# A hybrid decoder trunk: the attention layer in sixteen units of a quarter of the tokens and one head, and weights and rows loaded ahead of the stage borders

## Chip, cores and metric

One core of a Trainium2 chip runs the whole program as one launch. The metric is the device time of one execution in microseconds (us). All work is float32. Matrix products are made of three passes over operands that were split into a high and a low part (fp32r): high x high, high x low, low x high.

## What is computed

```python
def reference(x, ...):                      # x: 1 x 2048 x 1024
    x = x + gla_mixer(x, ...)               # layer 0
    x = x + hier_moe(x, ...)
    x = x + rglru_mixer(x, ...)             # layer 1
    x = x + hier_moe(x, ...)
    return rmsnorm(x, final_norm)

def gla_mixer(x, ...):                      # 4 heads, keys 128, values 256, chunks of 64 tokens
    q, k, v, g, lr = split(rmsnorm(x) @ w_in)
    log_a = log_sigmoid(lr @ w_alpha + b_alpha) / 16
    cum = cumsum(log_a within a chunk)
    q_in, k_in = q * exp(cum - mid), k * exp(mid - cum)
    o = causal(q_in @ k_in.T) @ v + (q * exp(cum)) @ state
    state = exp(last) * state + (k * exp(last - cum)).T @ v
    return (rmsnorm(o per head) * silu(g)) @ w_out

def hier_moe(x, ...):                       # 4 groups of 8 experts, hidden 256
    h = rmsnorm(x)
    group = argmax(h @ w_group); top 2 of its 8 experts by h @ w_expert
    return weighted sum of (silu(h @ w_gate) * (h @ w_up)) @ w_down over the two
```

`rglru_mixer` is a convolution over four tokens, two gates of 256 x 256 blocks, a linear recurrence over the tokens and two projections.

## The kernel before, in words

Seven stages run one after the other: `gla`, `project_and_route` (layer 0), `experts`, `lru`, `project_and_route` (layer 1), `experts`, `finish`. Each stage has its own memory, its own semaphores and a barrier at its end, and nothing of a stage is loaded before the stage begins. Every stage is written as one program for each engine (SyncE issues loads and stores, ScalarE, VectorE, TensorE, GpSimd the gathers), and each of them works strictly in the order of its lines; they meet through semaphores. SyncE first primes most semaphores (`m.prime`), so that loops may wait for an index below zero.

**gla** (line 264) works on two halves of 1024 tokens. At the start of a half all eight tiles of 128 tokens are loaded, normalised (`Norm`, squares and root on ScalarE, L259 the product on VectorE), transposed on TensorE (L685) and split into `hT_hi` and `hT_lo`; then come two low-rank projections `lr` (L693, 24 products each). Behind that is a loop over four heads. A head has two groups of 512 tokens:

- TensorE projects Q, K (24 products of 512 columns each, L710) and the decay logits (L714) for both groups. ScalarE copies Q and K out of PSUM and makes the softplus in four steps (L466 to L473); VectorE sums up (`sum_up`, L585 to L592); ScalarE makes five exponentials (L481 to L485); VectorE multiplies them with Q and K (`decay`, L596 to L612).
- Per tile TensorE makes values and gates together (24 products, L118 to L120 of `matmul3`), the scores (L747 to L751), and for the tile before the outputs and the update of the state (L725 to L728). ScalarE copies the values (L502) and squares the outputs (`square_o`, L417); VectorE takes the scores (L619 to L624), the outputs and the state (L629, L631).
- After four tiles the outputs are gated: silu (L517) and a root on ScalarE, the product on VectorE (L640); TensorE transposes them (L672, eight products), in the second tile of the next group, or at once for the second group of a head; ScalarE takes them (`take_oT`, L425), SyncE stores them.

The raw weights of a head lie in one buffer, `w_raw`: first Q and K (2048 columns a partition), split in ScalarE's L411 and VectorE's L544, then values and gates (4096 columns). Each head's weights are thus loaded and split twice, once in each half.

**project_and_route** projects with `w_out` (L118, weights split in four parts, L963), adds the residual, normalises, computes router logits and, on VectorE in small steps each of which waits for the one before, chooses experts and places each token in a list (`choose` 15 steps, `place_tokens` 14 steps, L1001 to L1034). **experts** loads the weights of 32 experts through two buffers, splits them (L1343, L1384) and runs over blocks of gathered rows. **lru** adds the two expert rows to x (L1747) and works in sixteen steps. **finish** adds the expert rows of the second MoE and normalises (L1967, L248), four tiles to an iteration of a loop.

Of the kernel before, what the change touches and what calls it, by code (L numbers as in the profile page):

```python
# [30 lines left out]
P = 128  # L31
BANK = 512
START = 4
DMA = 16
# [133 lines left out]

def stand(eng):


    eng.nop(nofuse=True)
# [91 lines left out]
def gla(nc, k, x_dram, norm_w, w_in, w_alpha, b_alpha, head_norm, oT_dram):  # L264
# [3 lines left out]

    with ExitStack() as ctx:
        m = Memory(nc, ctx, "gla")
        hT_hi = m.sb("hT_hi", [P, KD, TH], F32R)
        hT_lo = m.sb("hT_lo", [P, KD, TH], F32R)  # L280
        work = m.sb("work", [P, 4, D])
        q_k = m.sb("q_k", [P, 2 * GROUP])
        q_sb, k_sb = q_k[:, 0:GROUP], q_k[:, GROUP:]
        norm = Norm(m, k, work[:, 0:2], work[:, 2:4], q_k[:, 0:D])

        vg = work[:, 0:2].rearrange("p a (b c) -> p (a b) c", c=2 * DV)
        o_raw = work[:, 2].rearrange("p (a c) -> p a c", c=DV)
        gated = work[:, 3].rearrange("p (a c) -> p a c", c=DV)


# [10 lines left out]
        wal_in, wal = m.sb("w_alpha_in", [RANK, DK]), m.sb("w_alpha", [RANK, DK])  # L301
        bal_in, bal = m.sb("b_alpha_in", [P, 1]), m.sb("b_alpha", [P, 1])
        hn = m.sb("head_norm", [P, DV // P])
        lrT = m.sb("lrT", [RANK, TH])

        q_in, k_in, q_x, k_x, q_dec, k_dec = (m.sb(s, [P, NG, GROUP]) for s in (
            "q_in", "k_in", "q_x", "k_x", "q_dec", "k_dec"))
        tile_decay = m.sb("tile_decay", [P, NG, GT])
# [10 lines left out]
        oss = m.sb("oss", [P, GT])  # L319
        ostd = m.sb("ostd", [P, GT])  # L320
        orstd = m.sb("orstd", [P, GT])
# [6 lines left out]
        hT_ps_done, hT_hi_done, hT_lo_done = m.sem("hT_ps_done"), m.sem("hT_hi_done"), m.sem("hT_lo_done")  # L328
        small_in = m.plain("small_in")
        wlr_done, zeroed = m.plain("wlr_done"), m.plain("zeroed")  # L330
        wqk_in, wvg_in = m.plain("wqk_in"), m.plain("wvg_in")
        wqk_hi_done, wqk_lo_done = m.sem("wqk_hi_done"), m.sem("wqk_lo_done")
        wvg_hi_done, wvg_lo_done = m.sem("wvg_hi_done"), m.sem("wvg_lo_done")
        lr_ps_done, lrT_done = m.sem("lr_ps_done"), m.sem("lrT_done")
        qkz_ps_done = m.sem("qkz_ps_done")
        soft_steps = m.sem("soft_steps")
        cum_done, exps_done, group_done = m.sem("cum_done"), m.sem("exps_done"), m.sem("group_done")
        vg_ps_done, vg_done = m.sem("vg_ps_done"), m.sem("vg_done")
        sc_ps_done, sc_done = m.sem("sc_ps_done"), m.sem("sc_done")
        ou_ps_done = m.sem("ou_ps_done")  # L340
        o_raw_done, state_done = m.sem("o_raw_done"), m.sem("state_done")
        oss_done, ostd_done = m.sem("oss_done"), m.sem("ostd_done")
        og_done, oT_ps_done, oT_done = m.sem("og_done"), m.sem("oT_ps_done"), m.sem("oT_done")
        oT_stored = m.store("oT_stored")
# [6 lines left out]

        @block.sync
        def _(sp):
            m.prime(sp)

            def load_qk(h):
                sp.dma_start(wqk_raw[:, :, 0:DK], w_rows[:, :, bass.ds(h * DK, DK)]).then_inc(wqk_in, DMA)
                sp.dma_start(wqk_raw[:, :, DK:], w_rows[:, :, bass.ds(h * DK + KC, DK)]).then_inc(wqk_in, DMA)
                sp.dma_start(wal_in[:], w_alpha[:, bass.ds(h * DK, DK)]).then_inc(wqk_in, DMA)
                with nc.allow_non_contiguous_dma(reason="128 biases"):  # L360
                    sp.dma_start(bal_in[:], b_alpha.rearrange("(c o) -> c o", o=1)[bass.ds(h * DK, DK), :])\
                        .then_inc(wqk_in, DMA)

            def load_vg(h):
                sp.dma_start(wvg_raw[:, :, 0:DV], w_rows[:, :, bass.ds(h * DV + VC, DV)]).then_inc(wvg_in, DMA)
                sp.dma_start(wvg_raw[:, :, DV:], w_rows[:, :, bass.ds(h * DV + GC, DV)]).then_inc(wvg_in, DMA)

            for i in range(2):
                sp.dma_start(norm.x[:, i], x_dram[i * P:(i + 1) * P, :]).then_inc(x_in[i], DMA)
            sp.dma_start(norm.norm_w[:], norm_w.partition_broadcast(P)).then_inc(norm.norm_w_in, DMA)  # L370
            sp.dma_start(wlr_raw[:], w_rows[:, :, LC:LC + RANK]).then_inc(small_in, DMA)
            with nc.allow_non_contiguous_dma(reason="256 gains"):
                sp.dma_start(hn[:], head_norm.rearrange("(h p) -> p h", p=P)).then_inc(small_in, DMA)
            load_qk(0)
            sp.wait_ge(wqk_lo_done, nth(0))
            load_vg(0)
            with sp.Fori(0, HALVES) as half:
                for i in range(2, HT):
                    sp.wait_ge(norm.h_done, nth(half * HT + (i - 2)))
                    sp.dma_start(norm.x[:, i % 2], x_dram[bass.ds(half * TH + i * P, P), :])\  # L380
                        .then_inc(x_in[i % 2], DMA)
                with sp.Fori(0, HEADS) as h:
                    n = half * HEADS + h


                    sp.wait_ge(wvg_lo_done, nth(n))
                    load_qk((h + 1) % HEADS)
                    sp.wait_ge(wqk_lo_done, nth(n + 1))
                    load_vg((h + 1) % HEADS)
                    for g in range(NG):  # L390
                        sp.wait_ge(oT_done, nth(n * NG + g))
                        for e in range(DV // P):
                            sp.dma_start(oT_dram[bass.ds(h * DV + e * P, P),
                                                 bass.ds(half * TH + g * GROUP, GROUP)],
                                         oT[:, e]).then_inc(oT_stored, DMA)


                for i in range(2):
                    sp.dma_start(norm.x[:, i], x_dram[bass.ds(((half + 1) % HALVES) * TH + i * P, P), :])\
                        .then_inc(x_in[i], DMA)  # L400
            sp.wait_ge(oT_stored, nth_store(HALVES * HEADS * NG * (DV // P) - 1))
            sp.wait_ge(wqk_in, nth_dma(4 * HALVES * HEADS + 3))
            sp.wait_ge(wvg_in, nth_dma(2 * HALVES * HEADS + 1))
            for i in range(2):
                sp.wait_ge(x_in[i], nth_dma(HALVES * HT // 2))

        @block.scalar
        def _(act):
            def split_qk(n):
                act.wait_ge(wqk_in, nth_dma(4 * n + 3))  # L410
                nc.scalar.activation(wqk_hi[:], wqk_raw, ACT.Copy).then_inc(wqk_hi_done, 1)  # L411

            def square_o(i, t):

                act.wait_ge(oss_done, nth(t - 1))
                act.wait_ge(o_raw_done, nth(t))
                nc.scalar.activation(o_square[:], o_raw[:, i], ACT.Square,  # L417
                                     accum_out=oss[:, i:i + 1]).then_inc(oss_done, 1)
# [1605 lines left out]
```

## Time and profile before

| | us |
|---|---|
| median of three runs | 3212.1 (3206.96 to 3215.69) |
| the profiled execution | 3209.87 |
| its span | 3208.1 |
| gla ends | 868.6 |
| project_and_route (layer 0) ends | 1156 |
| experts (layer 0) ends | 1714 |
| lru ends | 2279 |
| project_and_route (layer 1) ends | 2557 |
| experts (layer 1) ends | 3096 |
| TensorE busy | 2677.0 (83%) |
| VectorE busy | 1824.7 (57%) |
| ScalarE busy | 1626.1 (51%) |
| GpSimd busy | 588.3 (18%) |
| DMA, busiest of 40 slices | 342 GB/s |

The ends are those of the last instruction of a stage; in gla the first transposes on TensorE start at 24.6. The mean granted clock of TensorE over the span is 0.925 of its full 2.4 GHz. PE is TensorE's matrix product, DVE is VectorE, ACT is ScalarE. A busy share is a mean over stages with different limits, so the table only says where to look.

### The profile page before, as it was taken

Reading aid. Unit: us, or ns where it says so; the run is one execution under the profiler, and the core shown is the slowest. Engines: PE = TensorE matmul, PEld = TensorE weight load, DVE = VectorE, ACT = ScalarE, POOL = GpSimd, SP = SyncE. Lnnn points to the kernel's source line nnn. Section 1 sums busy time; section 2 is a strip of 40 time slices with the busy share of each in tenths; the row PEclk is TensorE's granted clock in tenths of the full one; section 3 lists DMA queues with packets and bytes.
Section 4 is the critical chain, followed back from the end, with each engine's and each line's share of the span. In section 5 each row is a group of like instructions: output and inputs, shape, how many; then the busy total and the mean of one; then the engine's idle time right before and its main releaser. Section 6 shows DMA issues by size and latency. Waiting matters only on the chain. (4 is left out here: it accounts for less than half of the span.)

```text
span 3208.1 us, 43209 instructions
## 1 busy us (share of the span) xinstructions
PE 2677.0 (83%) x12246; PEld 2126.9 (66%) x12246; DVE 1824.7 (57%) x3426; ACT 1626.1 (51%) x2253; POOL 588.3 (18%) x795
## 2 busy tenths in 40 slices
PE   4999969999789949999993999999599588999940
PEld 3777756777678837777772777777488466777730
DVE  3444443434356656657653688886466667656645
ACT  3445444444334436556653666666344266555533
POOL 0000000000001134545450000000011144545420
PEclk9999979999989979999996999999799789999975
DMA  3111121111154359888876445422444299977857
GB/s 102 44 46 52 35 83 39 32 47 52 59 199 144 124 197 325 282 281 293 299 245 223 163 167 172 167 99 86 159 138 144 86 342 342 314 253 262 288 224 274
DMA packets 358416, 552.11 MB, mean 172 GB/s; under 512 B 32128, under 2 KB 273936, under 8 KB 354192
## 3 DMA queue, kind: packets, MB, share of 16 engines
q1 hardware_dynamic: 323296, 436.20, 41.1%
q0 software_dynamic: 32688, 105.99, 8.8%
q10 hardware_dynamic: 2304, 8.39, 0.6%
q8 instruction: 58, 0.95, 0.1%
q14 instruction: 70, 0.57, 0.0%
HBM read 428.29 MB, written 122.22 MB: 172 GB/s over the span
## 5 line engine op out<-in xcount | busy, mean ns | idle before, releaser
L1384 DVE TENSOR_TENSOR experts_gu_lo<-experts_gu_raw,experts_gu_hi 128x1024 fp32r<-128x1024 f32 x256 | 296.5, 1220 | 83.8 <-ACT experts_gu_hi L1343 82.1
L118 PE MATMUL experts_ps<-experts_gu_hi,experts_hT_hi 128*128 128x512 f32 x760 | 318.3, 419 | 0.5 <-DVE experts_hT_lo L1395 0.5
L1266 POOL DMA_INDIRECT experts_rows<-h_rows,experts_source_now x194 | 261.9, 1350 | 273.8 <-PE experts_ps L1436 136.7
L119 PE MATMUL experts_ps<-experts_gu_lo,experts_hT_hi 128*128 128x512 f32 x760 | 301.7, 397 | 0.0
L120 PE MATMUL experts_ps<-experts_gu_hi,experts_hT_lo 128*128 128x512 f32 x760 | 299.9, 395 | 0.0
L1343 ACT ACTIVATE experts_gu_hi<-experts_gu_raw 128x1024 fp32r<-128x1024 f32 x256 | 249.9, 1055 | 74.2 <-DMA experts_gu_raw<-in_moe_w_up 74.2
L892 POOL MEMSET route_empty<- 128x512 int32 x2 | 1.1, 549 | 1445.0 <-POOLq L160 1445.0
L118 PE MATMUL route_ps<-route_w_hi,route_src_hi 128*128 128x512 f32 x512 | 213.1, 416 | 60.6 <-DVE route_w_lo L963 60.6
L1395 DVE TENSOR_TENSOR experts_hT_lo<-experts_ps,experts_hT_hi 128x512 fp32r<-128x512 f32 x194 | 132.9, 686 | 225.1 <-ACT experts_hT_hi L1322 223.8
L118 PE MATMUL gla_ps<-gla_wvg_hi,gla_hT_hi 128*128 128x512 f32 x512 | 212.1, 414 | 0.0
L1335 ACT ACTIVATE experts_y<-experts_ps,experts_by_block 128x1024 f32<-128x1024 f32 x99 | 110.6, 1117 | 199.0 <-DMA y_rows<-experts_y,experts_target_now 198.8
L119 PE MATMUL route_ps<-route_w_lo,route_src_hi 128*128 128x512 f32 x512 | 207.7, 406 | 0.0
L120 PE MATMUL route_ps<-route_w_hi,route_src_lo 128*128 128x512 f32 x512 | 207.2, 405 | 0.0
L118 PE MATMUL experts_ps<-experts_wd_hi,experts_aT_hi 128*128 (+1 forms) x396 | 174.3, 440 | 34.2 <-DVE experts_aT_lo L1400 28.7
L120 PE MATMUL gla_ps<-gla_wvg_hi,gla_hT_lo 128*128 128x512 f32 x512 | 202.6, 396 | 0.0
L119 PE MATMUL gla_ps<-gla_wvg_lo,gla_hT_hi 128*128 128x512 f32 x512 | 201.6, 394 | 0.0
L1436 PE MATMUL experts_ps<-ident,experts_rows 128*128 128x128 f32 x776 | 122.5, 282 | 93.3 <-DMA experts_rows<-h_rows,experts_source_now 92.5
L1436 PEld LDWEIGHTS experts_ps<-ident,experts_rows 128*128 128x128 f32 x776 | 93.3, 143 | 137.1 <-issue 113.1
L120 PEld LDWEIGHTS experts_ps<-experts_gu_hi,experts_hT_lo 128*128 128x128 f32 x760 | 143.2, 188 | 35.2
L119 PE MATMUL experts_ps<-experts_wd_lo,experts_aT_hi 128*128 (+1 forms) x396 | 163.6, 413 | 0.0
L120 PE MATMUL experts_ps<-experts_wd_hi,experts_aT_lo 128*128 (+1 forms) x396 | 163.4, 413 | 0.0
L118 PEld LDWEIGHTS experts_ps<-experts_gu_hi,experts_hT_hi 128*128 128x128 f32 x760 | 144.1, 190 | 27.4 <-DVE experts_hT_lo L1395 0.7
(300 smaller groups left out, 6528.1 us busy)
## 6 DMA issues: line engine op xcount, KB each, us to landing
experts_gu_raw<-in_moe_w_gate SPq DMA_DIRECT2D x64, 1024.0 KB
experts_gu_raw<-in_moe_w_up SPq DMA_DIRECT2D x64, 1024.0 KB
experts_wd_raw<-in_moe_w_down SPq DMA_DIRECT2D x64, 1024.0 KB, 5.7
gla_w_raw<-in_gla_w_in SPq DMA_DIRECT2D x18, 1024.0 KB, 6.6
route_src<-oT_rows SPq DMA_DIRECT2D x32, 512.0 KB, 4.3
x_rows<-route_x_new SPq DMA_DIRECT2D x32, 512.0 KB, 2.9
h_rows<-route_h SPq DMA_DIRECT2D x64, 256.0 KB, 2.3
lru_y_ab<-y_rows SPq DMA_DIRECT2D x16, 1024.0 KB, 7.6
```

The source lines that it names most:

```text
L118: nc.tensor.matmul(out, w_hi, x_hi, start=first, stop=False)
L119: nc.tensor.matmul(out, w_hi, x_lo, start=False, stop=False)
L120: return nc.tensor.matmul(out, w_lo, x_hi, start=False, stop=last)
L892: pool.memset(empty[:, :, 1], 0)
L1266: pool.indirect_dma_start(rows[:, b], None, h_halves[b], bass.IndirectOffsetOnAxis(source_now[b][:].bitcast(U32), 0))\
L1335: nc.scalar.activation(y[:].rearrange("p (b c) -> p b c", b=2), ps[:, Y:Y + 2], ACT.Copy, scale=by_block[:, bass.ds(i + (LAG - 2), 1), 1]. ...
L1343: nc.scalar.activation(gu_hi[:, slot(e), of_part(c)], gu_raw[:, slot(e), of_part(c)], ACT.Copy)\
L1384: nc.vector.tensor_tensor(gu_lo[:, slot(e), of_part(c)], gu_raw[:, slot(e), of_part(c)], gu_hi[:, slot(e), of_part(c)].bitcast(F32), ALU.s ...
L1395: nc.vector.tensor_tensor(hT_lo[:, of_half(b)], ps[:, HT_ + b].rearrange("p (a c) -> p a c", c=P), hT_hi[:, of_half(b)].bitcast(F32), ALU. ...
L1436: last = nc.tensor.transpose(ps[:, HT_ + b, c * P:(c + 1) * P], rows[:, b, c * P:(c + 1) * P], k.ident[:])
```

## The change

`gla` is written anew and unrolled. It goes over sixteen units; unit u is quarter u // 4 of the tokens (512 of them, four tiles) and head u % 4.

- Only the first four tiles are normalised and transposed in front. The others follow one in each unit: in unit u, tile u + 4 is normalised at the end of the unit before, transposed after the first tile's scores, and split. `hT` has two buffers of a quarter each. The low-rank product of the next quarter stands in a quarter's last unit.
- Q and K of the next unit are projected at the end of a unit, its decay logits in the unit's second tile, its softplus and `sum_up` after the third tile. VectorE reads Q and K straight from PSUM. Output transposes stand in the second tile of the next unit; the silu covers all four tiles.
- Weights are loaded and split in every unit, so sixteen times each instead of eight. Values and gates are split in four parts of 1024 columns.
- gla's semaphores aren't primed.

TensorE's new order:

```python
for u in range(UNITS):                                   # 16
    ahead = u + GT
    for i in range(GT):                                  # 4 tiles
        t = GT * u + i
        values(t)
        if i == 1 and ahead < NT and u % HEADS == HEADS - 1:
            after(pe, hT_lo_done, ahead)
            low_rank(u // HEADS + 1)
        scores(t)
        if i:
            outputs(t - 1)
        if i == 0 and ahead < NT:
            transpose(ahead, Q)
        if i == 1:
            if ahead < NT:
                after(pe, hT_lo_done, ahead)
            if u:
                transpose_outputs(u - 1)
            if u + 1 < UNITS:
                decay_logits(u + 1)
    if u + 1 < UNITS:
        after(pe, oT_done, u - 1)
        project(u + 1, Q, 0, q_ps_done)
    outputs(t)
    if u + 1 < UNITS:
        project(u + 1, K, DK, k_ps_done)
```

VectorE's (ScalarE's mirrors it, with `square_o(t - 1)` ahead of `split_qk(u + 1)`, which stands ahead of `take_oT(u - 1)`; `soften(u + 1)` ahead of `mean_square` and `root_mean` of the next tile; then `gate(u)`, `decays(u + 1)`, `split_vg(u + 1)`, `square_o` and `root_o`):

```python
for u in range(UNITS):
    ahead = u + GT
    split_vg(u)
    if u:
        take_outputs(GT * u - 1)
    decay(u)
    if u:
        gate_outputs(u - 1)
    for i in range(GT):
        t = GT * u + i
        take_scores(t)
        if i:
            take_outputs(t - 1)
        if i == 0 and ahead < NT:
            take_hT(ahead, Q)
        if i == 1 and u + 1 < UNITS:
            split_qk(u + 1)
        if i == 2 and u + 1 < UNITS:
            sum_up(u + 1)
    if ahead + 1 < NT:
        normalise(ahead + 1)
```

TensorE, second tile of a group, before (group 1 of a head; `gla_work` holds values and gated outputs):

```order
L747 MATMUL gla_ps<-gla_q_in,gla_k_in 128x128 [waits gla_sc_done]
L749 MATMUL gla_ps<-gla_q_x,gla_k_x 128x64
L751 MATMUL gla_ps<-ident,gla_k_dec 128x128
L725 MATMUL gla_ps<-gla_work,gla_sT 128x256 [waits gla_o_raw_done,gla_state_done,gla_vg_done,gla_sc_done]
L726 MATMUL gla_ps<-gla_state,gla_q_dec 128x256
L728 MATMUL gla_ps<-gla_work,gla_kd 128x256
L757 ISA
L672 MATMUL gla_ps<-ident,gla_work 128x128 [waits gla_og_done]
L672 MATMUL gla_ps<-ident,gla_work 128x128 x7
L118 MATMUL gla_ps<-gla_wvg_hi,gla_hT_hi 128x512 [waits gla_vg_done]
```

and after, second tile of a unit:

```order
L756 MATMUL gla_ps<-gla_q_in,gla_k_in 128x128 [waits gla_sc_done,gla_group_done]
L757 MATMUL gla_ps<-gla_q_x,gla_k_x 128x64
L758 MATMUL gla_ps<-ident,gla_k_dec 128x128
L767 MATMUL gla_ps<-gla_vg,gla_sT 128x256 [waits gla_o_raw_done,gla_state_done,gla_vg_done,gla_sc_done]
L768 MATMUL gla_ps<-gla_state,gla_q_dec 128x256
L770 MATMUL gla_ps<-gla_vg,gla_kd 128x256
L776 MATMUL gla_ps<-ident,gla_gated 128x128 [waits gla_og_done,gla_hT_lo_done]
L776 MATMUL gla_ps<-ident,gla_gated 128x128 x7
L732 MATMUL gla_ps<-gla_lrT,gla_w_alpha 128x512 [waits gla_wqk_lo_done,gla_soft_steps,gla_lrT_done]
L118 MATMUL gla_ps<-gla_wvg_hi,gla_hT_hi 128x512 [waits gla_vg_done]
```

The decay logits (L732) moved in between the output transposes and the next tile's values, with a wait for the low part of the next unit's Q and K weights.

VectorE, from a unit's third tile to the next unit's decays, after:

```order
L614 SCALAR_TENSOR_TENSOR gla_cum<-keep,gla_z 128x512 [waits gla_exps_done,gla_vector_order]
L618 TENSOR_TENSOR gla_soft<-gla_cum 128x512 [waits gla_vector_order]
L619 TENSOR_TENSOR gla_to_end<-gla_cum 128x512
L651 COPY gla_kd<-gla_ps 128x128 [waits gla_sc_ps_done,gla_ou_ps_done]
L654 COPY_PREDICATED gla_sT<-causal,gla_ps 64x64 x2
L655 COPY gla_sT<-gla_ps 64x64
L660 COPY gla_o_raw<-gla_ps 128x256 [waits gla_ou_ps_done]
L662 SCALAR_TENSOR_TENSOR gla_state<-gla_state,gla_tile_decay,gla_ps 128x256 [waits gla_ou_ps_done]
L577 RECIPROCAL gla_rstd<-gla_std 128x1 [waits gla_std_done]
L579 SCALAR_TENSOR_TENSOR gla_h<-gla_x,gla_rstd,gla_gain 128x1024 [waits gla_hT_ps_done,gla_vector_order]
L599 TENSOR_TENSOR gla_wvg_lo<-gla_w_raw,gla_wvg_hi 128x1024 [waits gla_wvg_hi_done] x4
L660 COPY gla_o_raw<-gla_ps 128x256 [waits gla_ou_ps_done]
```

The sums of the next unit stand ahead of the fourth tile's scores, and the four parts of the value weights ahead of the last tile's outputs; before, sums, decays and the split stood at the head of a head, in front of its first scores.

At the stage borders:

- An arena (`Carry`, allocated once) holds in turn gla's first `hT` buffer, the raw `w_out` of a route stage, the raw gate and up weights of the experts, and lru's first `hT` buffer. With it, loads move ahead: `w_out` into gla's last quarter and lru's last four steps; the gate, up and down weights of experts 0 and 1 into the last two tiles of each route stage (`load_ahead`); lru's first x tiles, gain, small parameters, and first weights behind the last expert weights (`LruEarly`); finish's gain and six x tiles likewise (`FinishEarly`).
- gla no longer loads x tiles that nothing reads at its end.

```diff
 @block.sync                                             # lru
             for t in range(2):
-                load_x(t)
                 load_y(t)
-            sp.dma_start(gain[:], norm_w.partition_broadcast(P)).then_inc(gain_in, DMA)
-            load(wx, 0)
-            load(wg, 0)
             next_x(2)
-            load(wr, 0)
...
-                    sp.dma_start(par[:, :, at], v.rearrange("(c p) -> p c", p=P)).then_inc(par_in, DMA)
 @block.vector                                           # project_and_route
-            CHOOSE = 15
+            CHOOSE = 12
...
-            PLACE = 14
+            PLACE = 8
```

In the route stages the choice of experts masks the other groups by adding a large negative number instead of summing over groups, and the place in the list is worked out with shifts and an or of integers. `finish` is unrolled over its sixteen tiles.

## Rows read from the trace of the kernel before

**Rows 1.** Windows: stretch, us, busy us and count of PE, PEld, DVE, ACT, POOL, PEclk, DMA share, GB/s.
```profile
70.30:440.70 370.40, 350.04 (x1584) 279.75 (x1584) 156.30 (x368) 172.40 (x274) 0.00 (x0) 0.99 0.15 44
440.70:496.70 56.00, 29.59 (x114) 17.74 (x113) 21.31 (x32) 25.41 (x47) 0.00 (x0) 0.60 0.28 84
480.69:489.04 8.35, 8.34 (x24) 2.83 (x24) 0.00 (x0) 0.00 (x0) 0.00 (x0) 0.66 0.00 0
```

**Rows 2.** PE's waits of gla (us, times, longest), and windows of 4 us behind two.
```profile
PE gla_ps L672 <- DVE gla_work L640: 20.5, 8, 2.6
...
680.90:684.90 4.00, 3.97 (x15) 3.50 (x16) 0.00 (x0) 1.90 (x3) 0.00 (x0) 0.57 0.00 0
774.30:778.30 4.00, 3.98 (x22) 3.39 (x23) 0.00 (x0) 2.75 (x3) 0.00 (x0) 1.00 0.12 45
```

**Rows 3.** Timeline of PE in a head: start, us, instruction.
```profile
565.71 0.60 PE L725 MATMUL gla_ps<-gla_work,gla_sT 128*128 128x256 f32 x2
...
567.01 1.04 PE L672 MATMUL gla_ps<-ident,gla_work 128*128 128x128 f32 x8
...
573.48 0.38 PE L747 MATMUL gla_ps<-gla_q_in,gla_k_in 128*128 128x128 f32 x2
...
573.99 0.60 PE L725 MATMUL gla_ps<-gla_work,gla_sT 128*128 128x256 f32 x2
...
580.88 0.38 PE L747 MATMUL gla_ps<-gla_q_in,gla_k_in 128*128 128x128 f32 x2
```

**Rows 4.** Timeline of ACT in a head: start, us, instruction, idle time before it.
```profile
575.57 0.42 ACT L417 ACTIVATE gla_o_square<-gla_work 128x256 f32<-128x256 f32 x1 [1.30 <-DVE gla_work L629]
...
578.55 0.85 ACT L517 ACTIVATE gla_work<-gla_work 128x768 f32<-128x768 f32 x1
...
602.58 0.69 ACT L466 ACTIVATE gla_z<-gla_ps,gla_b_alpha 128x512 f32<-128x512 f32 x1 [0.45 <-PE gla_ps L714]
...
611.63 0.63 ACT L481 ACTIVATE gla_q_in<-gla_soft 128x512 f32<-128x512 f32 x1 [2.50 <-DVE gla_to_end L592]
...
634.09 1.90 ACT L411 ACTIVATE gla_wqk_hi<-gla_w_raw 128x2048 fp32r<-128x2048 f32 x1
```

**Rows 5.** Timeline of DVE in a head, and four parts of a split in experts.
```profile
607.86 0.43 DVE L585 TENSOR_SCALAR gla_z<-gla_z 128x512 f32<-128x512 f32 x1 [9.76 <-ACT gla_soft L473]
...
610.91 0.68 DVE L592 TENSOR_TENSOR gla_to_end<-gla_cum 128x512 f32<-128x512 f32 x1
...
613.96 0.69 DVE L596 TENSOR_TENSOR gla_k_x<-gla_k_x,gla_q_k 128x512 f32<-128x512 f32 x1 [2.36 <-ACT gla_e_chunk L485]
...
617.45 0.15 DVE L612 TENSOR_TENSOR gla_tile_decay<-gla_e_chunk 128x4 f32<-128x4 f32 x1
...
636.23 2.27 DVE L544 TENSOR_TENSOR gla_wqk_lo<-gla_w_raw,gla_wqk_hi 128x2048 fp32r<-128x2048 f32 x1
...
1168.27 4.63 DVE L1384 TENSOR_TENSOR experts_gu_lo<-experts_gu_raw,experts_gu_hi 128x1024 fp32r<-128x1024 f32 x4 [7.13 <-ACT experts_gu_hi L1343]
```

**Rows 6.** Stage borders, from timelines and waits of each engine, in order of time.
```profile
891.36 0.77 PE L118 MATMUL route_ps<-route_w_hi,route_src_hi 128*128 128x512 f32 x1 [24.15 <-DVE route_w_lo L963]
...
1147.52 0.22 DVE L1028 TENSOR_REDUCE route_rank_now<-route_at_rank 128x2 f32<-128x64 f32 x1
...
PE experts_ps L118 <- DVE experts_aT_lo L1400: 10.4, 6, 3.1
...
1726.44 1.23 DVE L1747 TENSOR_TENSOR lru_x<-lru_x,lru_y_ab 128x1024 f32<-128x1024 f32 x1 [11.67 <-DMA lru_gain<-in_lru_norm]
...
1752.73 1.23 DVE L1747 TENSOR_TENSOR lru_x<-lru_x,lru_y_ab 128x1024 f32<-128x1024 f32 x1 [4.72 <-DMA lru_x<-x_rows]
...
PE experts_ps L118 <- DVE experts_aT_lo L1400: 18.4, 8, 6.3
...
3104.76 1.22 DVE L1967 TENSOR_TENSOR finish_x<-finish_x,finish_y_ab 128x1024 f32<-128x1024 f32 x1 [23.01 <-DMA finish_x<-x_rows]
...
3132.41 1.28 ACT L248 ACT_TABLE_LOAD   x1 [4.00 <-DVE finish_x L1968]
```

More of the change, by code:

```diff
@@ L368, in _, with load_vg @@
[L368 to L370 removed]
+            def load_vg(u):
+                hd = u % HEADS
+                after(sp, wqk_lo_done, u)
+                for at, first in ((0, VC), (DV, GC)):
+                    sp.dma_start(wvg_raw[:, :, at:at + DV], w_rows[:, :, first + hd * DV:first + (hd + 1) * DV])\
+                        .then_inc(wvg_in, DMA)
@@ L373, in _ @@
                 sp.dma_start(hn[:], head_norm.rearrange("(h p) -> p h", p=P)).then_inc(small_in, DMA)
+            load_x(2)
             load_qk(0)
-            sp.wait_ge(wqk_lo_done, nth(0))
+            for t in range(3, GT + 1):
+                load_x(t)
             load_vg(0)
[L377 to L400, printed above, removed]
@@ new lines, in gate_outputs @@
+            def gate_outputs(u):
+                after(dve, ostd_done, u)
+                step(nc.vector.reciprocal(orstd[:], ostd[:]))
+                for i in range(GT):
+                    last = nc.vector.scalar_tensor_tensor(
+                        out=gated[:, i], in0=o_raw[:, i], scalar=orstd[:, i:i + 1], in1=gated[:, i],
+                        op0=ALU.mult, op1=ALU.mult)
+                last.then_inc(og_done, 1)
+            dve.wait_ge(gain_in, DMA)
+            normalise(0)
+            for t in range(GT):
+                if t + 1 < GT:
+                    normalise(t + 1)
+                take_hT(t, 2 * (t % 2))
+                if t == 0:
+                    dve.wait_ge(wlr_done, 1)
+                    nc.vector.tensor_tensor(wlr_lo[:], wlr_raw[:], wlr_hi[:].bitcast(F32), ALU.subtract)\
+                        .then_inc(wlr_done, 1)
+                if t == 1:
+                    split_qk(0)
@@ L871, in body @@
                 more = not (isinstance(t, int) and t >= NT - 2)
+                if not more:
+                    load_ahead(t - (NT - 2))
                 if more:
@@ L1614, in _ @@
             for n in range(STEPS):
+                if n == STEPS - LRU_BLOCKS:
+                    after(sp, gb_ps_done, n - 1)
+                    for a, rows in enumerate(w_out.rearrange("(a b p) c -> a p b c", a=len(out_early.landed), p=P)):
+                        sp.dma_start(out_early.raw[:, a], rows).then_inc(out_early.landed[a], DMA)
                 if n + GT + 2 < NT:
```

994 lines of the change are left out of this document (539 added, 455 removed).

## The prediction, before the changed kernel was run

> **What bounds the kernel now.** I read the span by stretches first. The GLA stage, which the change rewrites, ends at 868.6 of 3208.1 us, and inside it TensorE is the busy engine: between the first projection and the last transposes of the first half it works 350 of 370.4 us, so one group of 512 tokens and one head costs 370.4 / 8 = 46.3 us. Around that there are 70.3 us before the first projection and 56.0 us at the border of the halves, where TensorE works 29.6 us and its granted clock is 0.60 of 2.4 GHz on average; the first 24 low-rank products behind that border stand at 0.66 and take 8.35 [rows 1]. I then listed TensorE's waits: one of 2.6 us at the end of each head, eight in all, for the gated outputs; and I looked at the granted clock in the 4 us behind the six of them that lie inside a half. In four it is 0.57, 0.61, 0.61 and 0.66, in two 1.00 (one of each kind stands in [rows 2]). So a wait of 2.6 us is followed by the 1.2 GHz level in two of three cases, and that costs about 4 x 0.4 = 1.6 us more. The rest of the argument is a chain over three engines, for which I took single rows in order of time [rows 3 to 5], and the stage borders, where TensorE stands idle for other engines' first and last steps [rows 6].
>
> **The work of a unit.** Per tile TensorE issues scores (0.51), outputs (1.30) and the value and gate products; tile to tile is 7.40, so the 24 products take 5.6, and Q and K, 24 products each, take 5.6 each. The eight output transposes take 1.04 [rows 3]. The decay logits I put at 1.0, an estimate by two of the 0.60 rows, which move 256 columns each against its 512, with some overlap. Four tiles, Q, K, transposes and logits give 29.6 + 11.2 + 1.0 + 1.0 = 42.8; the change adds 1.04 of input transposes to twelve units and three times 5.6 of low-rank products between the units, which before stood in the borders. If TensorE never waited, a unit would take 43.8 against 46.3 and the borders would vanish. Two waits in the new order forbid that.
>
> **Wait a.** In tile 1 the new order has scores, outputs of tile 0, the transposes of the unit before, and then the logits of the next unit, which wait for the low part of its Q and K weights. TensorE arrives 0.51 + 1.30 + 1.04 = 2.85 after tile 1's scores began. ScalarE issues the square of tile 0 first, 2.09 after the scores began, and then, 0.42 later, the weights' high part (1.90); VectorE then takes the low part, 2.27 [rows 3 to 5]. That is 2.09 + 0.42 + 1.90 + 2.27 + 0.1 for the handover = 6.8. Wait a is 6.8 - 2.85 = 4.0 us, in 15 of 16 units. Everything on TensorE queues behind it. The load of these weights (issued a unit earlier) is no part of it.
>
> **Wait b.** Count from tile 2's scores. ScalarE squares tile 1 until 2.5, then the softplus of the next unit runs 5.28 (z at 602.58, VectorE's next step at 607.86) to 7.8; VectorE sums for 3.73 (607.86 to 611.59), to 11.5, and only then copies tile 3's scores and outputs (about 1.4 of the 2.09 above, an estimate) so that ScalarE squares tile 2 at 12.9 to 13.3; table load 1.28, gate 1.06 (by 0.85 for 768 columns), table load 1.28, to 17.0; the exponentials until VectorE can go on, 2.33, to 19.3 [rows 4, 5]. The four parts of the V and gate weights end on VectorE about 1.1 (ScalarE's first part, half of 1.90 and an overhead) + 4.63 later, at 25.1; the last tile's two output copies about 0.9, an estimate from VectorE's 512-column step of 0.69; the decays 3.64 (613.96 to 617.60), to 29.7 [rows 5]. TensorE needs 7.4 for tile 2's remaining work and tile 3's products, 0.5 + 1.3 + 5.6 + 1.3 + 5.6 for scores, outputs, Q, outputs, K, and 5.6 for the next tile 0: 27.3. Wait b, at the first scores of the next unit, is 29.7 - 27.3 = 2.4 us. The period, from tile 2's scores round to tile 2's scores, is 29.7, tile 0's scores and the input transposes 0.5 + 1.0, tile 1's products 5.6, its scores to the end of wait a 6.8, logits 1.0, tile 2's products 5.6: 50.3 with rounding, longer than the 46.3 of now.
>
> On these ScalarE steps the Trainium skill ("ScalarE: Activation LUTs", section "What ACT_TABLE_LOAD costs") says that every change of table set costs 1.28 us and a drain of 1.38 besides. The rows have only the 1.28: behind a load the next activation starts at once. By the page wait b, which holds four changes, would be 5.5 longer, and fifteen units 83 us longer.
>
> **The clock.** Wait a is longer than the 2.56 of the rows and wait b shorter. I take the fall in two of three of the first and one of three of the second: 15 x 1.6 = 24 us; bounds 0 and 30 x 1.6 = 48.
>
> **The sum for GLA.** Start: the first transposes need only x and the gain and no priming of semaphores, about 13 us after the start instead of the 24.6 of the stage table, an estimate; but VectorE takes the Q and K split ahead of tile 3's norm, so four tiles are ready at about 35, the low-rank product ends at 43, Q, logits and K at 55, softplus, sums and exponentials at 61, V's split at 67, decays at 71 (an estimate by the steps above, 6 us either way). From there 13.5 + 7.2 + 7.4 to tile 3's scores, 99; fifteen periods of 50.3 are 755; three low-rank products 17; less 4 for units without transposes and 5 for the last unit without wait a: 862; tail 10: 872. With the clock's 24 it ends at 896, against 868.6: **27 us slower**.
>
> **The borders** [rows 6]. (1) GLA to route 0: no unused x loads in front of the barrier, about 4 less, an estimate; the output weights have landed, but ScalarE still takes the source first and then 1.9 for part 0, VectorE 2.3, so the first product comes at 888 instead of 891.4: 3.5, likewise in route 1: 7. (2) The tail of each route stage: three place calculations lose six steps and two choices three, at 0.22 each with little overlap: 5, twice: 10. (3) Experts: the weights of experts 0 and 1 have landed when the stage begins. Before, the first down weights were loaded behind two experts' gate and up weights, and TensorE waited for their low part up to 3.1 in the first stage and up to 6.3, beside some 3, in the second; with a fall of the clock behind each I count 5 and 11. (4) LRU: the first addition starts at 1726.4 and waits for ten loads issued together; with only two y tiles to come it starts 6.5 earlier; the fourth tile waited 4.7 for x, whose load was behind eight small parameter loads on SyncE's queue, and the tile came 6.9 late: together 13.4. (5) Finish: three of four pairs of table loads at loop heads go, 3 x 2.56 = 7.7, and the first addition, 3104.8, waits for y alone, 3.3 less. Against this 3 MB and 3.5 MB of loads ride beside the last experts' gathers: 2 back. Other moved loads (output weights in the last GLA quarter, gate and up in the last two route tiles) I cost at nothing: the DMA engines are 0.15 busy beside GLA's heads [rows 1]; if uncovered, each MB would cost some 3 us, by the 342 GB/s of the profile's busiest slice. The sum is 4 + 7 + 10 + 16 + 13.4 + 11 - 2 = **59 us faster**; bounds 35 and 70.
>
> The profiled execution took 3209.9 us. 3209.9 + 27 - 59 = **3178**; against the median of 3212.1, a little above that execution, 1.1% faster.
>
> **The rivals.**
> *The forecast, 0.5.* Both waits, the clock between its bounds: 3150 to 3205.
> *Wait b is covered, 0.18.* Its margin, 29.7 against 27.3, rests on three estimates. Without it the clock's share is 16: 3178 - 15 x 2.4 - 8 = 3134. For: ScalarE and VectorE overlap adjacent steps by 0.1. Against: the path holds some 30 steps, and each handover costs as much.
> *The early loads bring half, 0.17.* The change does not do what it says: loads hidden earlier collide with gathers and stores, as where the first gathers wait now. 3178 + 30 = 3208.
> *The clock, the other side, 0.15.* Each of 30 waits brings 1.2 GHz and holds it as behind the border of the halves, where 24 low-rank products took 8.35 instead of 5.6 [rows 1], 2.7 more. Place: TensorE behind waits a and b. 3178 - 24 + 30 x 2.7 = 3235. It decides for slower from 68 / 30 = 2.3 us a wait (68 from 3154 to 3222). For: four of six waits of 2.6 us are followed by a fall, and wait a is longer than these. Against: after such a fall 15 products still ran in the 4 us, against 22 without, so it cost 1.6 and not more there [rows 2], and wait b is shorter. The Trainium skill ("TensorE: Matmul & The Clock Gate", section on HAM oscillation) has this as a rule against such a change: waits repeated in a loop bring the clock down each time. Two of six rows speak against "each time".
>
> **How the numbers follow.** About 0.3% is what a measurement of this kernel tells from no change, here 3202.5 to 3221.7. The forecast gives 0.46 faster and 0.04 same, the covered wait 0.18 faster, the half-paid borders 0.06, 0.08 and 0.03, the clock 0.02 same and 0.13 slower: 0.70, 0.14, 0.16. The range, 3125 to 3225, leaves out most of the clock case and the tail in which both waits are covered (3060).
>
> **What would show it.** Right: GLA's last output at about 896; per unit two waits of TensorE, 4.0 for the Q and K low part in front of the logits and 2.4 for the last decay step in front of tile 0's scores; period 50 to 52; the first LRU product some 13 earlier, finish some 11 shorter. Wrong: no wait in front of tile 0's scores, a period under 47, a GLA end under 850 or above 925, or experts no shorter.

## The result, and the profile after

The changed kernel takes 3154.9 us (median of 4 runs, 3152.4 to 3158.7) against 3211.9 (4 runs): 57 us less, a ratio of 0.982 (0.981 to 0.984). The profiled execution has a span of 3153.0 us. The forecast was 3178, with a range from 3125 to 3225. Two executions stand far outside, one of run 5's kernel (3543.3 us) and one of the kernel before beside runs 5 to 8 (8706.3 us), and no ratio below uses them. The page's busy times, to be read against the table of before:

```profile
PE 2664.5 (85%) x12246; PEld 2123.8 (67%) x12246; DVE 1819.5 (58%) x3169; ACT 1652.7 (52%) x2260; POOL 596.4 (19%) x795
```

They hardly moved: ScalarE has 27 us more, for the weights that are split twice as often, and VectorE 5 less, since the route stages' missing steps pay for its share of that. The gain isn't in busy time but in waits.

TensorE's waits in the attention stage, total us, times and the longest, answer [rows 2]:

```profile
PE gla_ps L732 <- DVE gla_wqk_lo L593: 61.5, 15, 4.8
PE gla_ps L756 <- DVE gla_k_dec L645: 23.4, 15, 1.7
```

These are waits a and b, fifteen each, as forecast; a has 4.1 on average (4.8 in the first, 4.0 to 4.1 in the others; forecast 4.0), b 1.6 (0.36 in the first, 1.62 to 1.66 in the other fourteen; forecast 2.4). The chain around wait b, which the prediction took from [rows 3 to 5], can be laid beside the forecast in one unit. Timelines of ScalarE, VectorE and TensorE of the changed kernel; tile 2's first scores start at 303.96, and from there the forecast counted:

```profile
306.06 0.42 ACT L505 ACTIVATE gla_o_square<-gla_o_raw 128x256 f32<-128x256 f32 x1 [1.30 <-DVE gla_o_raw L660]
...
316.70 0.42 ACT L505 ACTIVATE gla_o_square<-gla_o_raw 128x256 f32<-128x256 f32 x1 [1.82 <-DVE gla_o_raw L660]
...
318.53 1.06 ACT L498 ACTIVATE gla_gated<-gla_vg 128x1024 f32<-128x1024 f32 x1
319.59 1.28 ACT L483 ACT_TABLE_LOAD   x1
320.88 0.63 ACT L483 ACTIVATE gla_q_in<-gla_soft 128x512 f32<-128x512 f32 x1
```
```profile
311.73 0.43 DVE L611 TENSOR_SCALAR gla_z<-gla_z 128x512 f32<-128x512 f32 x1 [5.25 <-ACT gla_soft L476]
...
324.16 4.63 DVE L599 TENSOR_TENSOR gla_wvg_lo<-gla_w_raw,gla_wvg_hi 128x1024 fp32r<-128x1024 f32 x4 [5.65 <-ACT gla_wvg_hi L460]
...
332.78 0.28 DVE L645 COPY gla_k_dec<-gla_k_x 128x256 f32<-128x256 f32 x1
```
```profile
333.12 0.49 PE L756 MATMUL gla_ps<-gla_q_in,gla_k_in 128*128 128x128 f32 x2 [1.66 <-DVE gla_k_dec L645]
...
347.06 1.09 PE L732 MATMUL gla_ps<-gla_lrT,gla_w_alpha 16*128 16x512 f32 x2 [4.02 <-DVE gla_wqk_lo L593]
```

The sums start at 7.8 (forecast 7.8), tile 2's square at 12.7 (12.9), the exponentials at 16.9 (17.0), the V split ends at 24.8 (25.1), the decays at 29.1 (29.7); TensorE arrived at 27.5 (27.3). Behind each load of a table the next activation starts 0.01 to 0.02 later: nothing beyond the 1.28 us is to be seen.

The stages can be compared at places that both programs pass. Each delta is the time after less the time before, from TensorE's timelines, at the top from ScalarE's and for finish from VectorE's:

| place | before | after | delta | gained since the place above | forecast |
|---|---|---|---|---|---|
| last outputs of attention taken | 868.6 | 896.7 | +28.1 | -28.1 | -27 |
| first product of route 0 | 891.4 | 911.6 | +20.3 | 7.8 | 7.5 |
| first gathered rows of experts 0 | 1167.9 | 1169.1 | +1.3 | 19.0 | 5 |
| last block's down products begin, experts 0 | 1700.7 | 1700.7 | 0.0 | 1.3 | 5 |
| first product of lru | 1764.6 | 1753.1 | -11.5 | 11.5 | 13.4 |
| first product of route 1 | 2293.0 | 2279.9 | -13.1 | 1.6 | 3.5 |
| first gathered rows of experts 1 | 2569.5 | 2537.4 | -32.1 | 19.0 | 5 |
| the same place, experts 1 | 3082.5 | 3042.1 | -40.4 | 8.3 | 11 |
| first addition of finish | 3104.8 | 3060.5 | -44.2 | 3.8 | 3.3 |
| end | 3208.1 | 3153.0 | -55.1 | 10.9 | 7.7 |

The forecast's 2 us given back are not in the table. The attention stage lost what was forecast. The rest gave 83.2 us where 59.4 were forecast, and the difference lies in one line that stands twice: the route stages, 19.0 instead of 5, 28 us more, less some smaller shortfalls. Rows of TensorE in the route stages that answer [rows 6], first of the kernel before (all its waits for VectorE's chosen experts), then of the changed one:

```profile
PE route_ps L1131 <- DVE route_both L996: 18.9, 14, 5.0
PE route_ps L1100 <- DVE route_both L996: 12.6, 2, 6.3
```
```profile
PE route_ps L1160 <- DVE route_both L1062: 9.4, 2, 4.7
...
PE route_ps L1191 <- DVE route_both L1062: 5.9, 2, 3.0
```

Before, TensorE waited in fourteen places in front of the router logits, two of which are the tails' (5.0); the other twelve, 0.56 to 0.81 each, lie in the loops, and all twelve are gone. Behind six of the twelve TensorE's clock fell: its products of 512 columns show 0.63 us for some time instead of 0.39, which is the 1.2 GHz level. From router logits to router logits a tile takes 13.87 in the changed kernel. Before, a tile that ended in such a wait took 14.6 to 14.9, and the next one 15.5 where the clock fell and 14.0 where it did not.

### The profile page after: what moved, and what is told of

It reads as the page before. It is cut to its first block and busy times, and to the rows that moved or that the text cites. A ratio compares the mean times of both kernels' runs of the same rounds, so it can differ in the third digit from the quotient of the medians.

```text
span 3153.0 us, 41646 instructions
## 1 busy us (share of the span) xinstructions
PE 2664.5 (85%) x12246; PEld 2123.8 (67%) x12246; DVE 1819.5 (58%) x3169; ACT 1652.7 (52%) x2260; POOL 596.4 (19%) x795
## 5 line engine op out<-in xcount | busy, mean ns | idle before, releaser
L1439 DVE TENSOR_TENSOR experts_gu_lo<-carry_raw,experts_gu_hi 128x1024 fp32r<-128x1024 f32 x256 | 296.8, 1220 | 62.2 <-ACT experts_gu_hi L1398 60.7
L1398 ACT ACTIVATE experts_gu_hi<-carry_raw 128x1024 fp32r<-128x1024 f32 x256 | 250.2, 1056 | 46.9 <-DMA carry_raw<-in_moe_w_up 37.4
L118 PE MATMUL route_ps<-route_w_hi,route_src_hi 128*128 128x512 f32 x512 | 208.5, 407 | 51.7 <-DVE route_w_lo L1030 51.7
L493 ACT ACTIVATE gla_vg<-gla_ps 128x512 f32<-128x512 f32 x64 | 37.9, 593 | 260.9 <-PE gla_ps L120 260.7
L119 PEld LDWEIGHTS experts_ps<-experts_gu_lo,experts_hT_hi 128*128 128x128 f32 x760 | 143.5, 189 | 25.7
L651 DVE COPY gla_kd<-gla_ps 128x128 f32<-128x128 f32 x64 | 18.4, 287 | 244.9 <-PE gla_ps L758 244.9
## 6 DMA issues: line engine op xcount, KB each, us to landing
carry_raw<-in_moe_w_gate SPq DMA_DIRECT2D x64, 1024.0 KB, 10.9
carry_raw<-in_moe_w_up SPq DMA_DIRECT2D x64, 1024.0 KB, 12.7
```

What stands on the lines that cost most here:

```text
L118: nc.tensor.matmul(out, w_hi, x_hi, start=first, stop=False)
L119: nc.tensor.matmul(out, w_hi, x_lo, start=False, stop=False)
L493: nc.scalar.activation(vg[:, t % GT], ps[:, VG + t % 2], ACT.Copy).then_inc(vg_done, 1)
L1398: nc.scalar.activation(gu_hi[:, slot(e), of_part(c)], gu_raw[:, slot(e), of_part(c)], ACT.Copy)\
L1439: nc.vector.tensor_tensor(gu_lo[:, slot(e), of_part(c)], gu_raw[:, slot(e), of_part(c)], gu_hi[:, slot(e), of_part(c)].bitcast(F32), ALU.s ...
```

## The experiments

**1 to 3. The two waits of a unit.** The first moves the logits on TensorE, the second the sums on VectorE, the third is both.

```diff
@@ TensorE @@
+                    if i == 2 and u + 1 < UNITS:
+                        decay_logits(u + 1)
                     scores(t)
...
                         if u:
                             transpose_outputs(u - 1)
-                        if u + 1 < UNITS:
-                            decay_logits(u + 1)
@@ VectorE @@
-                    if i == 2 and u + 1 < UNITS:
+                    if i == 3 and u + 1 < UNITS:
                         sum_up(u + 1)
```

> The changed kernel, with the decay logits of the next unit moved on TensorE from behind the output transposes of tile 1 to behind the values of tile 2 (5.6 us of products later). Theory: TensorE's wait of 4.1 us for the low part of the Q and K weights is only an order in which it arrives early, and it goes in all 15 units, 61 us, with up to 20 us of low clock behind it; wait b stays at 1.6. That gives 3075 to 3094 us. Rival: the ScalarE and VectorE chain bounds the unit, so that the wait turns up in front of tile 0's scores instead: 3150 to 3158 us, with wait b grown to over 5 us.

> The changed kernel, with VectorE's sums of the next unit (five steps, 3.7 us) moved from ahead of tile 3's scores to behind tile 2's outputs. Theory: wait b (1.6 us in front of the first scores of a unit) hangs on the chain sums, tile 2's outputs, ScalarE's square, silu, exponentials, V split, decays; with square and silu off the sums' end it ends 3 us sooner, wait b goes, 15 x 1.6 = 23 us and a few us of clock: 3125 to 3135 us. Rival: the exponentials wait for the sums just as long, and the time stays within 3150 to 3160 us.

> Both moves together. Theory: the two waits are independent and both go, so a unit has only TensorE's own 43.8 us; 3154.9 - 61 - 23 - up to 25 of clock: 3046 to 3071 us, and the granted clock of the attention stage is near 1.00. Rival: without wait a the chain of ScalarE and VectorE is the longer one again and a wait b of some us comes back: 3080 to 3130 us.

Measured: 3062.5 us (3056.1 to 3064.1; ratio to before 0.954, 0.952 to 0.956), 3137.0 (0.977, 0.976 to 0.979) and 3031.9 (0.9445, 0.943 to 0.946). Waits of TensorE in the attention stage, of the first and of the second kernel:

```profile
PE gla_ps L756 <- DVE gla_k_dec L645: 23.4, 15, 1.7
```
```profile
PE gla_ps L732 <- DVE gla_wqk_lo L593: 61.5, 15, 4.8
```

Each move takes away its own wait and leaves the other as it was, to a tenth; in the third kernel neither stands. So the waits are independent, and both were a matter of order. The times missed their ranges, the first by 12 us below, the second by 2 above and the third by 14 below, and they do not add up exactly: 92.4 and 17.9 us alone, 123.0 together. Of attention alone the traces show 96.7 and 22.1, and 123.6 together; the rest is not explained. The first kernel ends the attention stage at 799.9 instead of 896.7, and of these 96.7 us the wait itself is 61.5: the other 35.2 are TensorE's clock, 2.35 us behind each wait a, not 1.6 behind two in three. (From unit to unit the first kernel takes 45.74; with the wait's 4.02 that would be 49.8, and the changed kernel takes 51.3 to 52.7.) The second ends it 22.1 sooner, its wait 23.4: behind wait b there was no low clock. Windows of 4 us of the changed kernel were read behind all thirty waits: 0.50 to 0.67 behind the fifteen waits a, 1.00 behind the fifteen waits b. Two of the one kind and one of the other (behind the five engines with their counts stand granted clock, DMA share and GB/s):

```profile
133.57:137.57 4.00, 4.00 (x7) 2.11 (x8) 0.00 (x0) 0.00 (x0) 0.00 (x0) 0.50 0.74 221
347.06:351.06 4.00, 4.00 (x9) 2.66 (x10) 0.00 (x0) 0.00 (x0) 0.00 (x0) 0.63 0.72 217
...
333.12:337.12 4.00, 4.00 (x24) 3.54 (x25) 3.76 (x11) 1.09 (x2) 0.00 (x0) 1.00 0.61 185
```

**4. The attention stage alone**, in a kernel that is otherwise the one before:

```diff
-        gla(nc, k, x[0], gla_norm[0], gla_w_in[0], ...
+        with ExitStack() as lent:
+            gla(nc, k, x[0], gla_norm[0], Carry(nc, lent), gla_w_in[0], ...
```

> The kernel before, with the changed kernel's attention function alone (its arena lent inside the stage, the early load of the output weights left out); every later stage as before. Theory: the attention rewrite by itself costs what the trace shows at its end, 896.7 against 868.6, so 3232 to 3248 us, slower than before; the gain of 57 us is made of the later stages and borders, some 85 us. Rival: the attention stage's length isn't what it costs, since the next stage starts as soon either way: 3195 to 3215 us.

Measured: 3227.4 us (3225.1 to 3233.7), ratio 1.0059 (1.0042 to 1.0075): slower, by 17 us, less than the 20 to 36 expected. Its first route product starts at 912.5 (before 891.4), so 5 of the 26 us by which attention ends later come back at the border already, where the new stage has no unused loads to wait for; the range had left that out. Another 6.8 came back in the first expert stage, whose code is that of before: from its first gathered rows to its last product it has 528.8 us here and 535.5 before. Why is not shown, so a gain of a few us that the table of places gives to an expert stage needs a run of its own. The rewrite of attention alone made the kernel slower; the rest of the change is worth 72 us, from 3227.4 to 3154.9.

**5 and 6. VectorE's small steps of the route stages.** The first undoes choice and place, the second the place alone.

```diff
-            CHOOSE = 12
+            CHOOSE = 15                                 # the first only
...
-                step(nc.vector.tensor_scalar(slot_int[:], rank_int[:], P - 1, ROW_SHIFT, ALU.bitwise_and,
-                                             ALU.logical_shift_left))
+                step(nc.vector.tensor_scalar(blk_int[:], rank_int[:], 7, None, ALU.logical_shift_right))
+                step(nc.vector.tensor_copy(blk[:], blk_int[:]))
...
-            PLACE = 8
+            PLACE = 14
```

> The changed kernel with VectorE's choice and place of the route stages as before (15 and 14 small steps a tile instead of 12 and 8). The two route stages became 19 us shorter each where 5 each were forecast. Theory: the missing nine steps work in every tile, not at the tail alone: with them VectorE is late for TensorE in every second tile, 0.8 us, and the clock falls behind it; the time goes to 3154.9 + 26 to 34 = 3181 to 3189 us. Rival: the steps are worth only the tail's 5 us a stage, and the rest comes from the loads moved ahead: 3163 to 3168 us.

> The changed kernel with the place steps alone as before (14 instead of 8), the choice as changed. VectorE waits 22 us in twelve tiles for TensorE in the changed route stage, 1.8 a tile, and six steps of 0.21 are 1.3 a tile. Theory (a threshold): the loop hides them, only the tail's three place calculations show, 3.8 us a stage: 3160 to 3166 us. Rival (steps count each time): two thirds of the 28 us come back, 3172 to 3178 us.

Measured: 3189.5 us for both (ratio to before 0.993, 0.992 to 0.994) and 3168.6 for the place alone (0.987, 0.985 to 0.988). The old choice and place together cost 34.5 us, half a us above the theory's 26 to 34 and far from the rival's; the trace has TensorE's waits in the loops again:

```profile
PE route_ps L1202 <- DVE route_both L1067: 17.4, 12, 5.0
...
PE route_ps L1171 <- DVE route_both L1067: 12.7, 2, 6.5
```

One of them in the timeline of TensorE, 0.78 us for 9 steps more a tile:

```profile
1051.92 1.95 PE L1202 MATMUL route_ps<-route_w_route,route_hT 128*128 128x36 f32 x16 [0.78 <-DVE route_both L1067]
```

The sixth lies between its two cases, 13.7 us above the changed kernel against 5 to 11 for a threshold and 17 to 23 for steps that count each time. From the first product to the start of TensorE's last rank product the first route stage has 238.0 us after the change, 243.9 with the old place, 252.7 with both old and 253.6 before. Of the 5.9 between the first two, 2.7 are the tail, whose waits are longer (4.28 and 6.01 instead of 2.95 and 4.68), and some 3 the loop. No wait there carries VectorE's name, but the timelines of TensorE and VectorE in run 6 show one all the same:

```profile
1048.15 1.95 PE L1199 MATMUL route_ps<-route_w_route,route_hT 128*128 128x36 f32 x16 [0.25 <-issue]
```
```profile
1047.82 0.19 DVE L1064 TENSOR_TENSOR route_both<-route_hot 128x32 bf16 x1
```

In every second tile TensorE stands idle for 0.10 to 0.29 us in front of the router logits, which the profile files under "issue". The logits then start 0.14 or 0.15 behind the end of VectorE's last step of the choice, exactly as behind the named waits of the kernel before. Such a tile takes 14.3 us instead of 13.87 and the next 13.96, 0.5 a pair, and six pairs make the 3 us. So VectorE is just late with six steps more, and more clearly late with nine. The clock marks the difference: it fell behind none of the eleven short waits in the loops of run 6, behind five of the eleven of 0.62 to 0.87 in run 5, and behind six of the twelve of 0.56 to 0.81 in the kernel before. The choice's steps, put on top of the place's six, cost more than those: 8.8 against 5.9 in this stage. There is a threshold, and run 6 lies just beyond it.

**7. The experts' first weights** loaded at the stage's start, as before:

```diff
-                if not more:
-                    load_ahead(t - (NT - 2))
...
+            load_gu(0)
+            sp.wait_ge(hT_ps_done, nth(1))
+            load_gu(1)
+            load_wd(0)
+            load_wd(1)
```

> The changed kernel, with the first two experts' weights loaded at the start of the expert stages, as before. Theory: the early loads are worth what the trace shows between the first gathered rows and the last product, 1.3 in the first expert stage and 8.3 in the second, and some 3 at the border: 3164 to 3172 us. Rival (the forecast's term): 16 us, 3169 to 3173 us. A second rival: the early loads delay the route stages' last stores and scatters as much as they give, and the time stays within 3150 to 3160 us.

Measured: 3169.9 us (3168.8 to 3172.7; ratio 0.987, 0.985 to 0.988), 15 more than with the early loads. That is the forecast's term of 16 within the scatter, but it lies in the theory's range too, so this run does not part the two. Waits of TensorE for the experts' second product, before, changed, and here:

```profile
PE experts_ps L118 <- DVE experts_aT_lo L1400: 28.7, 14, 6.3
```
```profile
PE experts_ps L118 <- DVE experts_aT_lo L1455: 15.9, 9, 3.1
```
```profile
PE experts_ps L118 <- DVE experts_aT_lo L1458: 31.7, 14, 8.6
```

The profile names the activations' low part as what came last. That is so because this step stands on VectorE behind the split of the down weights: in all 37 waits, the longest of 8.6 us among them, the product starts 0.8 to 0.9 us behind the end of such a split and 0.4 to 0.5 behind the activations' low part. The forecast took it so; that the split in its turn was late by the load was not measured apart.

**8. lru's first loads** at the stage's start, in the order of before:

```diff
-            lambda sp, wd_free: lru_early.load(sp, wd_free, x1, lru_norm[0], *lru_ws))
+            lambda sp, wd_free: None)
...
             for t in range(2):
+                load_x(t)
                 load_y(t)
+            sp.dma_start(gain[:], norm_w.partition_broadcast(P)).then_inc(gain_in, DMA)
```

> The changed kernel, with lru's x tiles, gain, parameters and first weights loaded at the stage's start in the order of before. Theory: 11.4 us come back, 6.6 in front of the first transposes and 4.8 before the fourth tile: 3163 to 3169 us. Rival: the weights loaded behind the last expert took as much from the last experts' gathers as they gave: 3153 to 3159 us.

Measured: 3168.9 us (3166.3 to 3169.9; 0.9865, 0.985 to 0.988), 14 more. The forecast had 13.4. TensorE's waits for lru's first normalised tiles, changed kernel and this one:

```profile
PE lru_ps L1992 <- DVE lru_h L1886: 37.3, 4, 22.9
```
```profile
PE lru_ps L2002 <- DVE lru_h L1896: 50.4, 4, 29.7
```

**9. What brings the low clock: the length of the wait, or what TensorE did before it?**

```diff
                     take_vg(GT * u + i)
+                    if i == 1 and u + 1 < UNITS:
+                        split_qk(u + 1)
                     if i:
                         square_o(GT * u + i - 1)
...
-                        if u + 1 < UNITS:
-                            split_qk(u + 1)
```

> The changed kernel, with ScalarE's high part of the next Q and K weights ahead of the square of tile 0's outputs instead of behind it. The low part is then ready some 5.0 us after tile 1's scores instead of 6.9, and wait a shrinks from 4.0 to 2.2 us in 15 units, 27 us. The question is the clock: all 15 waits a were followed by 1.2 GHz (2.35 us each beyond the wait itself), none of the 15 waits b of 1.65 us. If length decides, the shorter wait loses most of its fall, and the time is 3092 to 3112 us. If what TensorE did before decides (small products and transposes ahead of a, full ones ahead of b), the fall stays, and the time is 3122 to 3135 us.

Measured: 3124.7 us (3122.3 to 3130.4), within the second case. Waits of TensorE in this kernel, and 4 us behind one of the shorter waits a:

```profile
PE gla_ps L732 <- DVE gla_wqk_lo L593: 33.7, 15, 3.1
PE gla_ps L756 <- DVE gla_k_dec L645: 23.4, 15, 1.7
```
```profile
589.93:593.93 4.00, 4.00 (x8) 2.35 (x9) 0.00 (x0) 0.00 (x0) 0.00 (x0) 0.57 0.72 219
```

Attention ends 31.0 us sooner, the waits are 27.8 shorter: only 3.2 of the clock's 35 came back, though a wait now has 2.2 instead of 4.1. The 4 us behind the shorter waits have 0.54 to 0.80 in fourteen cases and 1.00 in one. Just ahead of wait a TensorE works on scores, outputs and transposes, small products all; just ahead of wait b on 24 products of 512 columns. That a wait of 2.2 us behind the one is followed by 1.2 GHz almost as surely as one of 4.1, and a wait of 1.65 behind the other never, speaks for what was done before as a condition. It is not settled, since no run had a wait of 2.2 us behind full products. And it can't be the whole condition: the waits of the route loops, 0.56 to 0.87 long, stand behind products of 512 columns too, and eleven of 23 were followed by a fall. What differs there is what comes behind the wait, sixteen router products of 36 columns, and the length counts at this place, as run 6 shows.

**10. The best version**, the third kernel with the output weights of the route stages split ahead of the first source tile:

```diff
-            split(0, 0, 0)
             for a in range(PARTS):
+                if a == PARTS - 1:
+                    split(0, 0, 0)
                 act.wait_ge(w_in[a], nth_dma(0))
```

> Both moves of the attention stage together (3031.9 us), and in the route stages the output weights, which have landed before the stage begins, are split ahead of the first source tile (ScalarE parts 0 to 2, VectorE parts 0 and 1) instead of behind it. Theory: ScalarE's 5.5 us of waiting for the source are used, the first product comes 2.9 us earlier and tile 0's products no longer wait for parts: 3 to 4 us a stage, 3023 to 3027 us. Rival: tile 0 is paced by something else behind the border (the second source tile, the residual), and the time stays within 3028 to 3035 us.

Measured: 3026.4 us (3023.0 to 3030.2, 5 runs), ratio to before 0.943 (0.941 to 0.945), in the theory's range. Against the third kernel's 3031.9 (3030.3 to 3035.4) it is 5.5 us or 0.2% faster. The executions of the two just do not overlap, but that is below the 0.3% that the prediction asks for, so the move's worth rests on the trace. The first route product starts at 782.8 instead of the third kernel's 787.9; 1.9 of these 5.1 us it was ahead at attention's end already, which no edit explains, so 3.2 are the move's. TensorE's waits in front of the first products went from 51.7 (both stages of the changed kernel) to 45.5, 3.1 a stage.

## Why the prediction was right, and where it was off

- The forecast was 23 us too long, and the time lies in its range. The attention stage came out to a microsecond by luck, as two errors cancel in it; the miss lies in the route stages.
- **The work of a unit** held: without waits the third kernel goes through attention with TensorE busy 717 of 731 us. Windows of the stage, the third kernel's first and then the changed kernel's:

```profile
41.00:772.00 731.00, 717.42 (x3334) 572.96 (x3332) 386.27 (x813) 415.89 (x629) 0.00 (x0) 0.99 0.29 89
```
```profile
41.00:897.00 856.00, 756.13 (x3333) 595.23 (x3331) 385.92 (x813) 418.13 (x629) 0.00 (x0) 0.94 0.25 76
```

- **Wait a**: 4.0 forecast, 4.1 measured, and by run 1 it was worth its full length.
- **Wait b**: 2.4 forecast, 1.6 measured. The chain was 0.6 shorter and TensorE 0.2 later than forecast. The rival in which it is covered did not come, but it was near.
- **The clock**: 24 us forecast for both waits; by runs 1 and 2 it was 35 behind a and none behind b. Taking two in three from [rows 2] was wrong for a: all fifteen were followed by 1.2 GHz. The rival that prices every wait at 2.7 us was nearly right for a (2.35) and wrong for b. The rule of the Trainium skill ("TensorE: Matmul & The Clock Gate", section on HAM oscillation) is that waits repeated in a loop bring the clock down each time. Its example has waits of some 3 to 5 us. The waits a, of 4.0 to 4.8, agree with it, 15 of 15 in this trace; the waits b, shorter than the example's, had no fall in any of 15.
- **The sum for attention**: 896 forecast, 896.7 measured. Two errors cancel in it: 13 us too much for wait b (15 x 2.4 against 23.4), and 11 too little for the clock with 1.5 too little for wait a.
- **The borders**: the step that failed is the second, "the tail of each route stage", 5 us a stage. It looked at the last three tiles alone, and took for granted that the loop is TensorE's. In the loop VectorE's small steps were in the way too: 12 waits, and the clock behind six of them. Measured: 34.5 us for the steps (run 5) instead of 10. Experts (15, run 7, for 16) and lru (14, run 8, for 13.4) were right. Finish and the borders have no run of their own; by the table of places finish gave 14.7 for 11: beside the three pairs of table loads one of the two in the first tile went too, and 0.1 to 0.3 us in each other tile. Runs 7 and 8 got back 15 and 14 us by undoing early loads, as much as the forecast had for them, so "the early loads bring half" is refuted.
- **The table loads**: the Trainium skill's drain of 1.38 beside 1.28 ("ScalarE: Activation LUTs", section "What ACT_TABLE_LOAD costs") would have made wait b some 5.5 us longer, and it came out 0.8 shorter than by the rows. The rows were the better price.

## What to carry to other kernels

When an engine order is written anew, follow each wait to where it could stand one step later: here one line moved by 5.6 us of products is worth 92 us, more than the whole change, whose rewritten stage by itself had made the kernel slower. A chain of small steps on another engine has to be priced in every turn of a loop, by asking whether the busy engine has any short wait there that ends with that chain, even of under 1 us, and even where the profile puts no name to it, as in run 6; the share of a stage's busy time hides such waits. And a wait of the engine with the gated clock can cost more than its length: behind the waits a the clock took over half of the wait again, behind the waits b nothing.

## What the runs showed of the hardware

Behind small products, a wait of TensorE of 2.0 to 3.1 us (run 9) or of 4.0 to 4.8 was followed by the 1.2 GHz level in 29 of 30 cases. Each fall cost 1.5 to 3.2 us, which is a unit's length less that of run 1's kernel and less the wait. A wait of 1.65 us behind 24 products of 512 columns was not followed by it in any of 14 cases, nor was the one of 0.36. In the route loops shorter waits stood ahead of such a fall, and there the wait comes behind full products and ahead of the router's sixteen products of 36 columns: waits of 0.56 to 0.87 us in eleven of 23 cases (the kernel before and run 5), waits of 0.10 to 0.29 in none of eleven (run 6). TensorE's timeline of the kernel before:

```profile
1006.09 1.95 PE L1131 MATMUL route_ps<-route_w_route,route_hT 128*128 128x36 f32 x16 [0.77 <-DVE route_both L996]
...
1009.13 0.63 PE L119 MATMUL route_ps<-route_w_lo,route_src_hi 128*128 128x512 f32 x1
```

At 2.4 GHz that last product, of 512 columns, shows 0.39 to 0.40. Windows of the two loops, before and changed, show the mean clock of 0.97 with these waits and 0.99 without:

```profile
932.30:1129.00 196.70, 187.97 (x971) 155.97 (x971) 128.18 (x555) 86.70 (x146) 24.97 (x26) 0.97 0.41 134
```
```profile
951.80:1136.00 184.20, 180.55 (x966) 152.36 (x965) 106.68 (x431) 86.67 (x146) 24.96 (x26) 0.99 0.53 177
```
